# Reordering the S5 mixer's set-up: three B sets, turn tables from coarse and fine steps, parameters turned first

## The reference, cut to what matters

```python
c_act = jax.nn.silu(c)
shift1, scale1, gate1, shift2, scale2, gate2 = jnp.split(c_act @ ada_w[l] + ada_b[l], 6, axis=-1)
h = modulate(rms_norm(x, norm1_g[l]), shift1, scale1)
...
dt = jnp.exp(log_dt)[:, None]              # 64 groups, 64 states, 16 channels each
mag = jnp.exp(lr * dt)
ab_re, ab_im = mag * jnp.cos(li * dt), mag * jnp.sin(li * dt)
f_re = ((ab_re - 1) * lr + ab_im * li) / (lr * lr + li * li)
f_im = (ab_im * lr - (ab_re - 1) * li) / (lr * lr + li * li)
bb = f * b                                 # complex, [group, state, channel]
s_t = ab * s_{t-1} + bb u_t                # complex diagonal state, 256 steps
y = Re(C s) + d_skip * h
g = gelu(y); mix = g * sigmoid(g @ w_glu + b_glu)
```

## Time and profile before

| | us |
|---|---|
| median of 3 runs | 1293.61 |
| lowest, highest | 1289.32, 1295.51 |
| the profiled execution | 1292.06 |
| its span in the trace | 1290.3 |
| busy: TensorE, VectorE, ScalarE | 1246.6, 857.1, 604.6 |

### The profile page before, as it was taken

The page is one execution under the profiler, slowest core; times in us unless marked ns, Lnnn a source line. Parts: engine busy times, 40 slices in busy tenths (PEclk is TensorE's granted clock), DMA queues, the critical chain, the costliest instruction groups (busy, mean ns, idle before and its releaser), DMA issues.

```text
span 1290.3 us, 25331 instructions
## 1 busy us (share of the span) xinstructions
PE 1246.6 (97%) x10936; PEld 1164.3 (90%) x10936; DVE 857.1 (66%) x1173; ACT 604.6 (47%) x781; POOL 50.2 (4%) x67
## 2 busy tenths in 40 slices
PE   5989999999999999999999999999999999999997
PEld 4667899999966489999999999999998999999997
DVE  6999678886537776768456655447459666666443
ACT  5845633433335565543445434336334545544342
POOL 5300000000000000000000000000000000000000
PEclk8969999999999999999999999999999999999998
DMA  9965478987652928655565554455455434655452
GB/s 262 315 217 174 163 258 299 326 293 256 209 180 96 295 86 278 217 173 165 165 208 177 178 180 147 156 186 161 134 164 160 135 131 131 202 189 194 143 177 74
DMA packets 219705, 247.03 MB, mean 191 GB/s; under 512 B 5872, under 2 KB 209088, under 8 KB 219616
## 3 DMA queue, kind: packets, MB, share of 16 engines
q1 hardware_dynamic: 211616, 218.63, 52.2%
q0 software_dynamic: 7648, 26.86, 6.1%
q10 hardware_dynamic: 352, 0.23, 0.1%
HBM read 244.66 MB, written 1.05 MB: 190 GB/s over the span
## 4 chain that ended last, share of the span: by engine, by line
PE 87%; DVE 7%; ACT 2%; DMA 2%; issue 1%; ACTq 0%; DVEq 0%
PE PS L1746 86%; ACT PARTS L592 1%; DVE ARENA L1154 1%; DMA RING<-in_ada_w 0%; DMA H<-in_s_log_dt 0%; DMA RING<-in_mla_w_uq 0%; DVE X L1158 0%; DMA RING<-in_w_in 0%; DVE ARENA L1262 0%; DVE PARTS L1012 0%; PE PS L2375 0%; DVE ARENA L1324 0%; DVE WL L1034 0%; DVE ARENA L1265 0%; DVE SQ L995 0%
## 5 line engine op out<-in xcount | busy, mean ns | idle before, releaser
L1746 PE MATMUL PS<-PARTS 128*128 128x256 f32 (+3 forms) x3608 | 839.8, 283 | 0.0
L1746 PEld LDWEIGHTS PS<-PARTS 128*128 128x128 f32 (+1 forms) x3608 | 619.3, 189 | 1.4 <-issue 0.9
L1034 DVE TENSOR_TENSOR WL<-RING,PARTS 128x2048 fp32r<-128x2048 f32 (+2 forms) x189 | 387.3, 2053 | 236.3 <-ACT PARTS L592 236.1
L1746 PE MATMUL PS<-HH,WL 128*128 128x256 f32 (+3 forms) x1832 | 520.9, 284 | 1.9 <-DVE PARTS L1003 0.9
L1746 PE MATMUL PS<-HH,PARTS 128*128 128x256 f32 (+3 forms) x1832 | 518.6, 283 | 0.0
L592 ACT CAST PARTS<-RING 128x2048 fp32r<-128x2048 f32 (+2 forms) x189 | 324.0, 1716 | 290.9 <-DMA RING<-in_w_ffn_out 66.8
L1746 PEld LDWEIGHTS PS<-HH,WL 128*128 128x128 f32 (+1 forms) x1832 | 345.1, 188 | 7.8 <-issue 4.9
L1746 PEld LDWEIGHTS PS<-HH,PARTS 128*128 128x128 f32 (+1 forms) x1832 | 344.4, 188 | 0.4
L1746 PE MATMUL PS<-PARTS,WL 128*128 128x256 f32 (+1 forms) x832 | 236.9, 285 | 0.8 <-DVE PARTS L1645 0.5
L1746 PEld LDWEIGHTS PS<-PARTS,WL 128*128 128x128 f32 x832 | 158.1, 190 | 2.7 <-issue 1.8
L1746 PE MATMUL PS<-ARENA 128*32 128x63 f32 (+8 forms) x864 | 59.2, 272 | 4.3 <-issue 3.1
(11 more groups left out here) (348 smaller groups left out, 992.8 us busy)
## 6 DMA issues: line engine op xcount, KB each, us to landing
RING<-in_w_ffn_in SPq DMA_DIRECT2D x44, 1024.0 KB, 5.1
RING<-in_ada_w SPq DMA_DIRECT2D x32, 1024.0 KB, 8.6
RING<-in_ffn_w_gate SPq DMA_DIRECT2D x22, 1024.0 KB, 5.3
RING<-in_ffn_w_up SPq DMA_DIRECT2D x22, 1024.0 KB, 5.2
RING<-in_w_in SPq DMA_DIRECT2D x20, 1024.0 KB, 5.2
ARENA<-in_ada_w POOLq DMA_DIRECT2D x16, 1024.0 KB, 7.3
RING<-in_ffn_w_down SPq DMA_DIRECT2D x16, 768.0 KB, 4.5
RING<-in_w_ffn_out SPq DMA_DIRECT2D x16, 768.0 KB, 4.2
```

What stands on the lines that cost most here:

```text
L1034: V.tensor_tensor(WL[:, u % SLOTS, 0:w], RING[:, u % SLOTS, 0:w], WH[:, u % SLOTS, 0:w].bitcast(fp32), SUB)\
L1746: return nc.tensor.matmul(o, lhsT, rhs, start=start, stop=stop)
```

## The change

SyncE loads the late constants ahead of unit 8 instead of unit 2, and VectorE waits for them only before the GLU. ScalarE's three parameter loads change places.

The three parameter rows are turned by TensorE as soon as `dt` is there, and the small arithmetic runs on 128 partitions by 32 columns (`LT`). B set 0 is B itself and uses `b_blocks(0)` on BRAW; the factor that was in the B sets stays with C. So VectorE makes B sets 1 to 3, one power lower each, and the last step's output takes C set 0 and the state of its own chunk. The filters are three taps, not four, and the skip weights are a matrix of their own (`SKIP`), so `taps` has no matmuls with the identity.

The tables are the sum of 8 coarse and 8 fine turns for each pair (`TURNS`), added out to 64 with one pass, reduced with one more, and the absolute value is taken with an integer mask.

C set 0 stands before the modulated input on VectorE, C sets 1 to 3 behind it, ahead of the first `turned_in`. On ScalarE `std(0)` stands behind the last row copy. On TensorE `stat(0)` stands right behind the transposes of x, `ada_rows(4)` behind `b_u(3)`, and `y_of` waits for the states only after skip and taps.

```diff
-                if u == 2:
+                if u == 8:
                     sp.dma_start(CN[:, C_LATE:], A["consts"][:, C_LATE:]).then_inc(S["late_loaded"], 16)
...
-            c_compact()
-            b_blocks(0)
-            row_copy(0)
-            std(0)
-            b_blocks(1)
+            b_blocks(0)
+            meta_copy()
+            b_blocks(1)
+            c_compact()
+            row_copy(0)
+            bt_out(0)
+            row_copy(1)
+            b_blocks(2)
+            bt_out(1)
+            row_copy(2)
+            b_blocks(3)
+            bt_out(2)
+            row_copy(3)
+            std(0)
+            bt_out(3)
             nc.scalar.preload_act_table_set("trig_and_small")
-            row_copy(1)
-            bt_out(0)
-            b_blocks(2)
-            row_copy(2)
-            bt_out(1)
-            b_blocks(3)
-            row_copy(3)
-            bt_out(2)
-            bt_out(3)
             shift(0, ADA_SHIFT1)
...
+            for k in range(1, CHUNK):
+                b_set(k)
+
+            m, f = by_pair(COS), by_pair(SIN)
+            fine, coarse = T_FINE, T_COARSE
+            part = [TURNS[:, r, :].rearrange("p (k j) -> p k j", j=8) for r in range(8)]
...
+            for g, steps_of in enumerate((coarse, fine)):
+                V.tensor_tensor(part[3 * g], steps_of, turn, MUL)
+                V.tensor_tensor(part[3 * g + 1], steps_of, low_part, MUL)
+                ins = V.tensor_tensor(part[3 * g + 2], steps_of, high_part, MUL)
+            link(ins)
+            link(V.tensor_scalar(TURNS[:, 0:4:3, :], TURNS[:, 0:4:3, :], MAGIC, MAGIC, ADD, SUB))
+            link(V.tensor_tensor(TURNS[:, 2:6:3, :], TURNS[:, 2:6:3, :], TURNS[:, 0:4:3, :], SUB))
+            link(V.tensor_tensor(TURNS[:, 2:6:3, :], TURNS[:, 2:6:3, :], TURNS[:, 1:5:3, :], ADD))
...
+            link(V.tensor_tensor(by_step, part[2].unsqueeze(3).broadcast_to([P, PAIRS, 8, 8]),
+                                 part[5].unsqueeze(2).broadcast_to([P, PAIRS, 8, 8]), ADD))
+            link(V.tensor_scalar(m, f, MAGIC, MAGIC, ADD, SUB))
+            link(V.tensor_tensor(f, f, m, SUB))
+            V.tensor_scalar(m.bitcast(i32), f.bitcast(i32), 0x7FFFFFFF, None, ALU.bitwise_and).then_inc(S["turn_cos"], 1)
...
             scaled(0, GS[:, 0, :], H, "norm_scaled")
...
+            c_set(1)
             dve.wait_ge(S["bt_ready"], 2 * CHUNK)
-            for k in range(2):
+            dve.wait_ge(S["bd_exp"], CHUNK)
+            for k in range(2, 4):
                 c_set(k)
...
-            dve.wait_ge(S["bd_zero"], 1)
+            dve.wait_ge(S["c_pow"], 4)
             for kt in range(4):
                 turned_in(kt)
-            c_set(2)
-            c_set(3)
...
                         for q in range(4):
                             rows = slice(32 * q, 32 * q + 32)
-                            ins = mm(KTAPS[rows, kt, :, :], BD[:, i, 4 * kt + q, :], CTD[:, :, i, kt, rows], i == 0, i == 1)
-                        if i == 0:
-                            for q in range(4):
-                                rows = slice(32 * q, 32 * q + 32)
-                                mm(KTAPS[rows, kt, 0, :], ident[rows, rows], KWD[rows, kt, 0, rows], False, False)
+                            ins = mm(KTAPS[rows, kt, :, :], BD[:, i, 4 * kt + q, :], CTD[:, 0:CHUNK - 1, i, kt, rows], i == 0, i == 1)
...
-                for d in range(CHUNK):
-                    mm(y[:, :, d:], KW4[d][:, kt, :], u[:, :, 0:CHUNK - d], d == 0, False)
+                mm(PS[:, 5 + kt % 2, 0:SEQ], SKIP[:, kt, :], H[:, kt, 0:SEQ], True, False)
+                for d in range(CHUNK - 1):
+                    mm(y[:, :, d:CHUNK - 1], TAPS[d][:, kt, :], u[:, :, 0:CHUNK - 1 - d], False, False)
+                pe.wait_ge(S["s_done"], kt + 1)
...
-            ada_rows(4)
             for kt in range(4):
                 b_u(kt)
+            ada_rows(4)
             ada_rows(5)
             ada_rows(6)
             for kt in range(4, KT):
```

More of the change, by code:

```diff
@@ L182, in build @@
         POW, at = arena(at, 2 * CHUNK, PAIRS)
+        CSETS = [t[:, 2 * i:2 * i + 2, :, :] for t in (CSET_EARLY, CSET_LATE) for i in range(2)]
         WPOW, at = arena(at, 2 * CHUNK, PAIRS)
@@ L663, in _ @@
-            nc.scalar.activation(LROW[0:PAIRS, 11, :], LROW[0:PAIRS, 9, :], ACT.Sin, scale=-1.0, bias=hpi[0:PAIRS])\
-                .then_inc(S["lrow_act"], 1)
+            act.wait_ge(S["lrow_dve"], 1)
+            nc.scalar.activation(LAM[:, 0, :], LT[:, 3, :], ACT.Exp).then_inc(S["lrow_act"], 1)
+            nc.scalar.preload_act_table_set("trig_and_small")
+            for b in range(2):
+                act.wait_ge(S["xt_ready"], b + 1)
+                nc.scalar.copy(X[:, 2 * b:2 * b + 2, NMETA:], PS[:, b, :].rearrange("p (m t) -> p m t", m=2)).then_inc(S["res_ready"], 2)
@@ new lines, in _ @@
+            act.wait_ge(S["lrow_dve"], 2)
+            nc.scalar.activation(LT[:, 13, :], LT[:, 6, :], ACT.Sin).then_inc(S["lrow_act"], 1)
+            nc.scalar.activation(LT[:, 14, :], LT[:, 7, :], ACT.Sin, scale=-1.0, bias=hpi).then_inc(S["lrow_act"], 1)
+            act.dma_start(BF[:, :], A["b_forget_2"].rearrange("a h -> h a")).then_inc(S["bf_loaded"], 16)
+            for b in range(2, 4):
+                act.wait_ge(S["xt_ready"], b + 1)
+                nc.scalar.copy(X[:, 2 * b:2 * b + 2, NMETA:], PS[:, b, :].rearrange("p (m t) -> p m t", m=2)).then_inc(S["res_ready"], 2)
@@ L737, in k_out @@
                         rows = slice(32 * q, 32 * q + 32)
-                        ins = nc.scalar.copy(KWD[rows, 4 * b:4 * b + 4, :, rows], KTAPS[rows, 4 * b:4 * b + 4, :, :])
+                        ins = nc.scalar.copy(KWD[rows, 4 * b:4 * b + 4, 1:, rows], KTAPS[rows, 4 * b:4 * b + 4, :, :])
                     ins.then_inc(S["k_used"], 1)
@@ L1225, in _ @@
[L1225 to L1226 removed]
+            L = [LT[:, r, :] for r in range(24)]
             def power(i, k):
                 return POW[:, i * CHUNK + k, :]
[L1231 to L1234 removed]
@@ L1280, in _ @@
+            dve.wait_ge(S["ct_used"], 1)
+            dve.wait_ge(S["dve_step"], steps[0])
+            c_set(0)
             dve.wait_ge(S["tr_ready"], 1)
-            dve.wait_ge(S["late_loaded"], 16)
             V.tensor_copy(VEC[:, :], PS[:, 6, 0:SEQ]).then_inc(S["tr_used"], 1)
@@ L2045, in _ @@
             nc.tensor.transpose(PS[:, 4, 0:KT], CROW[:, :], ident[0:KT, 0:KT]).then_inc(S["cact_ready"], 1)
+            pe.wait_ge(S["lrow_act"], 1)
+            for r in range(3):
+                ins = nc.tensor.transpose(PS[:, 6, r * PAIRS:(r + 1) * PAIRS], LROW[0:PAIRS, r, :], ident[0:PAIRS, 0:PAIRS])
+            ins.then_inc(S["lam_ready"], 1)
             pe.wait_ge(S["x_loaded"], 16)
@@ L2070, in _ @@
             ada_rows(0)
-            stat(0)
-            ada_cols(0)
-            ada_rows(1)
             def bt_of(k):
@@ L2088, in _ @@
             bt_of(0)
+            ada_rows(1)
+            ada_cols(0)
+            bt_of(1)
             pe.wait_ge(S["vrow_loaded"], 16 * (len(VROWS) + 4))
@@ L2093, in _ @@
             ins.then_inc(S["tr_ready"], 1)
-            for k in range(1, 3):
-                ada_cols(k)
-                ada_rows(k + 1)
-                bt_of(k)
+            ada_rows(2)
+            ada_cols(1)
+            bt_of(2)
+            ada_rows(3)
+            ada_cols(2)
             ada_cols(3)
```

233 lines of the change are left out of this document (104 added, 129 removed).

## The result

The changed kernel takes 1297.50 us (median of 16 runs, 1293.03 to 1308.98) against 1293.09 for the kernel before (16 runs, 1288.51 to 1297.68): ratio 1.0041, interval 1.0022 to 1.0060. It is a little slower, by 4.4 us. The profiled execution of the changed kernel is the fastest of its 16: 1293.03 us, span 1291.2, only 1.0 over the profiled one of before. This has to be kept in mind when its stages are added up.

The account below looks back on a forecast made before the run. The prediction took TensorE to bound the kernel, VectorE deciding only until 69.4 us. Ring +1.9, clock fall +5.8 and taps -2.1 made +5.6 on 1292.06: 1297.7 us, range 1287 to 1303.

Parts of the forecast that it names:

- (1) VectorE: VectorE's work before `b_u(4)`: products of the first four `turned_in` end at 66.6 us against 69.4, saving beside TensorE's work.
- (2), (3) Unit 7 and `b_u(0)`: Late constants moved: TensorE meets `ada_w` unit 7 at 43.2 us; through ScalarE's chores `b_u(0)` starts at 50.8, 2.2 earlier.
- rival B: Before `b_u(0)`: ScalarE's queue, not unit 7, sets its start; 2.5 us on top of the fall, 1300.2; chance 0.16.
- (4) The fall of the clock: TensorE's 2.9 us gap before `b_u(0)` lowers the clock for the first group and `ada_rows(4)`: 5.8 us of 7.2 taken.
- rival A: TensorE before `b_u(0)`: the clock keeps its level through the gap; sum -0.2, 1291.9 us; chance 0.18.
- (5) The ring: Four load slots: units 12 and 13 issued late, so `b_u(4)` at 71.5 us against 69.61 with the clock kept, +1.9.
- (6) The second group: `b_u(4)` to `b_u(7)` on TensorE stay at granted clock 0.50: 0; other end -6.2 us if the clock is full.
- rival C: Clock full in both groups of small matmuls, `ada_rows(6)` perhaps raising it before the second: 1285.7 us; chance 0.12.
- the forecast's doubt about it: First group on TensorE: the skill's rule would win the clock back, but 13.85 us of small matmuls read 0.50 throughout.
- (7) Taps: Taps on TensorE lose the four 32 x 32 skip matmuls per tile and shrink to 96 columns: -2.1 us, -1.5 to -2.6.
- (8) Outputs: `y_of` up to the GLU: same columns in another order, may start before the states, TensorE nearly full: 0.
- the sign of being right: First GLU matmul at 126 to 127 us, named among the signs that would show the forecast right.

Follow-up runs that it names:

- vector_slow: The changed kernel with five unused passes of 1024 columns on VectorE ahead of the first `turned_in`: 1298.86 us, ratio 1.0063 to the kernel before.
- std_early: The changed kernel with `std(0)` moved behind the first B copies and the trigonometric table load behind the second: 1292.92 us, ratio 1.0007 to the kernel before.
- small_filler: The changed kernel with 6 filler matmuls of 128x256 between the last transposes and `b_u(0)`: 1296.06 us, ratio 1.0031 to the kernel before.
- rows_first: The changed kernel with only `ada_rows(4)` put back ahead of `b_u(0)`: 1290.01 us, ratio 0.9975 to the kernel before.
- before_rows_behind: The kernel before with only `ada_rows(4)` moved behind `b_u(3)`, nothing else of the change: 1303.25 us, ratio 1.0079 to the kernel before.
- warm_gap: The changed kernel with 14 filler matmuls of 128x256 between the last transposes and `b_u(0)`: 1298.03 us, ratio 1.0039 to the kernel before.
- late_back: The changed kernel with the late constants loaded again between units 1 and 2 of the modulation's weights: 1297.92 us, ratio 1.0060 to the kernel before.
- c_sets_late: rows_second with C sets 2 and 3 moved back behind `turned_in(3)` on VectorE: 1289.23 us, ratio 0.9969 to the kernel before.
- paced_load: c_sets_late with GpSimd's last load for the first FFN issued only when the one before it has landed: 1287.12 us, ratio 0.9966 to the kernel before.
- rows_second: std_early with `ada_rows(4)` behind `b_u(0)` instead of `b_u(3)`: 1291.34 us, ratio 0.9988 to the kernel before.
- rows6_behind: The changed kernel with `ada_rows(6)` and the taps behind `b_u(7)`: 1296.00 us, ratio 1.0030 to the kernel before.
- vector_slow_rows_first: rows_first with five unused passes on VectorE ahead of the first `turned_in`: 1294.61 us, ratio 1.0020 to the kernel before.

## Why the prediction held, and where it did not

The forecast was 1297.7 and the median is 1297.5. By its own steps:

- **(1) VectorE** 66.6: the C sets end at 62.2, and with 4.9 for the products that makes 67.1; in the trace they wait 1.99 us more for the slow first group and end at 69.1. That the saving buys nothing is shown by vector_slow. Right.
- **(2), (3) Unit 7 and `b_u(0)`**: 43.2 and 50.8 forecast, 43.5 and 51.30 measured. std(0) and two table loads are on the path, as the forecast had it; std_early takes them off. Right. Of rival B the condition came nearly true, as ScalarE's queue and unit 7 set the last row copy within 0.3 us of each other, but not its price of 2.5 us.
- **(4) The fall of the clock**: the gap is 2.96 (2.9 forecast), the clock falls at 52.7 (0.85 in the microsecond from 52, 0.50 from 53) and the group and `ada_rows(4)` lose 5.0 + 1.2 = 6.2 for the 5.8 taken. Right on TensorE's timeline; rival A needed the filler to come true. As a price at the end of the span, 5.8 is not borne out: without the fall, small_filler's median is only 1.4 lower.
- **(5) The ring**: unit 13 lands 8.5 us after `ada_rows(4)` (8.2 forecast), `ada_rows(6)` takes 3.5 at the low level (2.9). The forecast has `b_u(4)` at 71.5 + 5.8 = 77.3, measured 79.30. The mechanism is right, and rows_first with before_rows_behind show it; the size is 2.0 short.
- **(6) The second group: wrong.** "I keep it there: 0" was taken, and in the profiled execution it was nearly its other end: -5.9. The clock came back 0.7 us into the group, behind `ada_rows(6)`, which is half of rival C. It did so too in before_rows_behind, std_early, small_filler, warm_gap and late_back. In vector_slow, whose order on TensorE is the same and whose passes nobody waits for, it did not, and the run took 1299.04:

```profile
80.63:94.49 13.86, 13.86 (x260) 13.74 (x256) 8.53 (x16) 0.00 (x0) 0.00 (x0) 0.50 0.59 191
```

  The level of this group is thus not a fixed number of the kernel, and a term of 0 or of -6 for it is no forecast; a chance of each would have been, and the prediction gave none to a fall in the first group alone. The rule of the Trainium skill (TensorE: Matmul & The Clock Gate, What's actually happening), that activity releases the throttle, does not fit these 13.86 us at 0.50; the forecast's doubt about it holds.
- **(7) Taps**: -2.1 taken; with the wait for their copies -1.8 here and, in rows_first, 86.00 to 89.59 = 3.6 us against 6.2, -2.6. Right in its bounds. That the copies behind the taps would now be waited for (0.75 us) was not seen.
- **(8) Outputs: +2.3 instead of 0.** A stall of 2.46 us in `ada_rows(9)` and a low clock behind it (0.94 over the stage) stand where the kernel before had stalls of 1.63 and 1.43.

So the ring and the fall in the first group, (4) and (5), came as forecast and make the change slower up to `b_u(4)`. That the total is 0.2 us off is luck. In the profiled execution (5), (6) and (8) missed by +2.0, -5.9 and +2.3, `ada_rows(7)` and (8) gained 1.2 with the clock that was back, the taps were 0.3 short, and the rest of the span gave 2.1: +1.0 for the +5.6 forecast, and a GLU start at 124.05 where 126 to 127 was named as the sign of being right. The median's 4.4 is that of other draws; the 16 runs have mean granted clocks of 0.977 to 0.984, the profiled one among the highest, and which groups fell in the others is not recorded. And the sum took a microsecond ahead of the GLU for a microsecond at the end. For kernels that start the GLU earlier than the kernel before, the table shows that part of it is lost again.

## What to carry to other kernels

A step that frees ring slots belongs ahead of the point where the load queue runs dry, not where it suits the engine's other work: ask of every moved step what its end lets start, and when that lands. Time saved on an engine counts only if the next wait is not already in place behind it; add work to the suspected engine in both orders to see where it counts. And a start that comes 8 us earlier can be worth 4: read the rest of the span too, and look there for transfers that now collide, new waits and a lower clock.

## What the runs showed of the hardware that was not expected

- The same gap of 1.55 us ahead of group 1 left the clock at 1.00 in c_sets_late and lowered it in paced_load, two kernels that differ only behind the GLU. From 48.5 to 54 us, of the one and of the other:

```profile
48.50:54.00 5.50, 3.95 (x82) 2.24 (x80) 5.47 (x10) 5.50 (x11) 5.22 (x3) 1.00 1.10 348
```

```profile
48.50:54.00 5.50, 4.33 (x72) 3.05 (x76) 5.14 (x8) 5.50 (x10) 5.43 (x3) 0.69 1.10 348
```

In all, a gap of 1.55 us was followed by a full clock in rows_second, c_sets_late and, up to its stall, std_early, and by a fall in paced_load and before_rows_behind; the gap of 2.96 was followed by a fall in all four kernels that have it (the change, late_back, vector_slow, rows6_behind).

- The stalls called "issue" recur at the same places of TensorE's program: 132 records into group 2 in rows_first, rows_second, c_sets_late and paced_load, 1.8 to 2.7 us each, and each with a fall of the clock near it that costs more than the stall. Fillers ahead moved a stall up by nearly their own number of records: in the changed kernel it stands 259 records behind the start of `b_u(4)`, in `ada_rows(7)`; with 6 fillers (12 records) at 248 and with 14 (28 records) at 232. They do not come each time: vector_slow and vector_slow_rows_first, with the order of the change and of rows_first on TensorE, have none there. Their cause was not tested.
